# The RWKV preparation of a hybrid diffusion step: sums of squares by dense products, full-width reciprocals, weights asked for earlier

## The reference

```python
kk = heads(k * k_k)
kk = kk / jnp.maximum(jnp.linalg.norm(kk, axis=-1, keepdims=True), 1e-12)
for d in range(2):                       # forward and backward scan
    w_raw = w0[d] + jnp.tanh(wd[:, :, d]) @ w2[d]
    decay = jnp.exp(-jnp.exp(-jax.nn.softplus(-w_raw) - 0.5))
    a = jax.nn.sigmoid(a0[d] + ad[:, :, d] @ a2[d])
    k_d = heads(k * (1 + (a - 1) * k_a))
    y_d, s_d = _wkv7_scan(r_h, decay, k_d, v_h, kk, a, s0, reverse=(d == 1))
```

## Time and profile before

| | |
|---|---|
| median of 3 runs | 2838.48 us |
| the profiled execution | 2838.06 us, span 2836.3 us |
| PE, DVE, ACT busy | 94%, 51%, 25% of the span |
| mean granted TensorE clock | 0.952 of full speed |
| the RWKV part | about 1260 to 1840 us |
| the three scans with a preparation | from about 1377, 1516 and 1660 us |

### The profile page before, as it was taken

How to read it: one execution, slowest core, us unless ns; L and a number is a source line. 1 busy time by engine, 2 the same in 40 slices (tenths; PEclk the granted TensorE clock), 3 DMA queues, 4 the chain that set the end, 5 groups by cost and what they waited for, 6 DMA issues and landing times. The chain is left out here.

```text
span 2836.3 us, 51388 instructions
## 1 busy us (share of the span) xinstructions
PE 2653.5 (94%) x21182; PEld 2520.2 (89%) x21182; DVE 1437.2 (51%) x2751; ACT 703.8 (25%) x1341; POOL 87.6 (3%) x158
## 2 busy tenths in 40 slices
PE   5999999999999799987979797988999999999998
PEld 3999999999999799845767676788999999999998
DVE  4754555555533866217584848444633333333344
ACT  3311111111112311124444444222311111111113
POOL 0000000000000000000202021200000000000000
PEclk8999999999999899987888888999999999999999
DMA  7222222222210222242021212051111111111101
GB/s 281 67 81 78 82 70 83 69 83 83 83 38 1 62 79 94 69 189 65 32 64 40 64 40 65 13 177 44 61 45 38 44 37 44 44 34 40 44 22 68
DMA packets 215861, 192.73 MB, mean 68 GB/s; under 512 B 64755, under 2 KB 184350, under 8 KB 215710
## 3 DMA queue, kind: packets, MB, share of 16 engines
q1 hardware_dynamic: 206224, 165.31, 18.6%
q10 hardware_dynamic: 9486, 25.26, 3.3%
HBM read 158.42 MB, written 32.11 MB: 67 GB/s over the span
## 5 line engine op out<-in xcount | busy, mean ns | idle before, releaser
L129 PE MATMUL ff_ps<-h_hi,ff_wlo 128*128 128x384 f32 x2112 | 715.2, 339 | 7.9 <-DVE h_lo L483 4.7
L130 PE MATMUL ff_ps<-h_lo,ff_whi 128*128 128x384 f32 x2112 | 705.8, 334 | 0.0
L131 PE MATMUL ff_ps<-h_hi,ff_whi 128*128 128x384 f32 x2112 | 705.5, 334 | 0.0
L684 DVE TENSOR_TENSOR ff_s<-ff_ps,ff_s 128x384 f32<-128x384 f32 x132 | 73.6, 557 | 688.6 <-PE ff_ps L131 686.4
L129 PEld LDWEIGHTS ff_ps<-h_hi,ff_wlo 128*128 128x128 f32 x2112 | 396.9, 188 | 11.8 <-DVE h_lo L483 7.8
L130 PEld LDWEIGHTS ff_ps<-h_lo,ff_whi 128*128 128x128 f32 x2112 | 396.9, 188 | 0.0
L131 PEld LDWEIGHTS ff_ps<-h_hi,ff_whi 128*128 128x128 f32 x2112 | 396.5, 188 | 0.0
L129 PE MATMUL ff_ps<-ff_uhi,ff_wlo 128*128 128x384 f32 x1056 | 353.9, 335 | 9.1 <-DVE x L695 9.1
L131 PE MATMUL ff_ps<-ff_uhi,ff_whi 128*128 128x384 f32 x1056 | 352.9, 334 | 0.0
L130 PE MATMUL ff_ps<-ff_ulo,ff_whi 128*128 128x384 f32 x1056 | 352.8, 334 | 0.0
L622 ACT ACTIVATE ff_s<-ff_ps 128x384 f32<-128x384 f32 x132 | 64.9, 492 | 752.8 <-PE ff_ps L131 752.8
(11 more groups left out here) (281 smaller groups left out, 3339.9 us busy)
## 6 DMA issues: line engine op xcount, KB each, us to landing
ff_n<-w_mod ACTq DMA_DIRECT2D x64, 384.0 KB, 3.2
ff_raw<-ffn_w_gate SPq DMA_DIRECT2D x44, 512.0 KB, 4.0
ff_raw<-ffn_w_up SPq DMA_DIRECT2D x44, 512.0 KB, 4.0
ff_raw<-ffn_w_down SPq DMA_DIRECT2D x44, 512.0 KB, 4.5
md_w<-w_mod SPq DMA_DIRECT2D x3, 4096.0 KB, 30.7
pj_raw<-w_in SPq DMA_DIRECT2D x19, 512.0 KB, 4.1
z_dram<-pj_zo SPq DMA_DIRECT2D x15, 576.0 KB, 2.9
rw_rkv<-z_dram SPq DMA_DIRECT2D x12, 576.0 KB, 4.9
```

Source lines behind the costliest of these rows:

```text
L129: pe.matmul(out, w_lo, x_hi, start=start, stop=False)
L130: pe.matmul(out, w_hi, x_lo, start=False, stop=False)
L131: return pe.matmul(out, w_hi, x_hi, start=False, stop=stop)
L684: dve.tensor_tensor(hid[:, t % 2, :], ps[:, 2 + t % 2, 0:CW], silu[:, t % 2, :], ALU.mult)\
```

## The change

`ss_c` becomes one product of the 128x128 block of ones (as loaded operand) with 384 columns of squares. So the sums come out already spread over the 64 channels of their head, 128x384. `wide` and the three `kk_c` items on PE are gone. The clamp, the square root and the reciprocal now work at full width: three clamps of 128x384, one `Sqrt` of 128x1152, three reciprocals of 128x384. The tables are written anew, with `sqrt` in step 5, `inv_0` in slot 1 of step 6, `inv_1` and `inv_2` in the two slots of step 7. SP asks for the small weights behind the block round trip, ahead of `gate_g2` and the big rows. PE and DVE wait for the three rows at the start of every pair's jobs, not of the first alone.

```diff
-PREP_PE = {0: ("a0_0", ), 1: ("a0_1", ), 2: ("ss_0", "ss_1"), 3: ("ss_2", ), 4: ("a0_2", ), 5: ("w0_0", ), 6: ("w0_1", ),
-           7: ("kk_0", ), 8: ("kk_1", ), 9: ("kk_2", ), 10: ("w0_2", ), 11: ("a1_0", ), 12: ("a1_1", ), 13: ("a1_2", ),
-           14: ("w1_0", ), 15: ("w1_1", ), 16: ("w1_2", )}
+PREP_PE = {0: ("a0_0", ), 1: ("a0_1", ), 2: ("ss_0", ), 3: ("ss_1", ), 4: ("ss_2", ), 5: ("a0_2", ), 6: ("w0_0", ), 7: ("w0_1", ),
+           8: ("w0_2", ), 9: ("a1_0", ), 10: ("a1_1", ), 11: ("a1_2", ), 12: ("w1_0", ), 13: ("w1_1", ), 14: ("w1_2", )}
...
             if name.startswith("ss"):
                 self.act_t.wait(pe, "sq")
-                j = int(name[-1])
-                last = head_sums(pe, self.sb, bank, rw.sq[:, :], range(j * NC, (j + 1) * NC))
+                c = int(name[-1])
+                last = pe.matmul(bank[:, 0:CW], self.sb["cst"][:, C_BLK:C_BLK + P], rw.sq[:, c * CW:(c + 1) * CW], start=True, stop=True)
...
-                t.did(name, act.activation(rw.inv[:, :], rw.inv[:, :], ACT.Sqrt))
+                t.did(name, act.activation(rw.sq[:, :], rw.sq[:, :], ACT.Sqrt))
...
-                ins = dve.tensor_scalar(rw.inv[:, six], self.ps[:, self.ITEMS.index(name) % 2, six], 1e-24, None, ALU.max)
+                ins = dve.tensor_scalar(rw.sq[:, cols], self.ps[:, self.ITEMS.index(name) % 2, 0:CW], 1e-24, None, ALU.max)
             elif kind == "inv":
                 self.act_t.wait(dve, "sqrt")
-                ins = dve.reciprocal(rw.inv[:, :], rw.inv[:, :])
-            elif kind == "wide":
-                t.wait(dve, "inv")
-                ins = widen(dve, rw.sq[:, :], rw.inv)
+                ins = dve.reciprocal(rw.sq[:, cols], rw.sq[:, cols])
             elif kind == "kk":
-                self.pe_t.wait(dve, name)
-                ins = dve.tensor_tensor(rw.kk[:, cols], self.ps[:, self.ITEMS.index(name) % 2, 0:CW], rw.kk[:, cols], ALU.mult)
+                t.wait(dve, f"inv_{c}")
+                ins = dve.tensor_tensor(rw.kk[:, cols], rw.sq[:, cols], rw.kk[:, cols], ALU.mult)
...
         back(0)
         back(1)
+        if more:
+            ready.pe_t.wait(sp, Prep.ITEMS[-1])
+            prep.sync_weights(sp)
...
-        else:
-            for sem in ready.z_in:
-                pe.wait_ge(sem, 16)
+        for sem in ready.z_in:
+            pe.wait_ge(sem, 16)
```

More of the change, by code:

```diff
@@ L1297, in others @@
         self.sq = sbuf("sq", [P, T])
-        self.inv = sbuf("inv", [P, 2 * NT])
         self.rkv = sbuf("rkv", [P, 3, T])
@@ L1348 @@
 PP = {n: i for i, n in enumerate(("w0_0", "w0_1", "a0_0", "a0_1", "k_k", "k_a", "r_k", "ln_w", "ln_b", "one_ka"))}
-PREP_PE = {0: ("a0_0", ), 1: ("a0_1", ), 2: ("ss_0", "ss_1"), 3: ("ss_2", ), 4: ("a0_2", ), 5: ("w0_0", ), 6: ("w0_1", ),
-           7: ("kk_0", ), 8: ("kk_1", ), 9: ("kk_2", ), 10: ("w0_2", ), 11: ("a1_0", ), 12: ("a1_1", ), 13: ("a1_2", ),
-           14: ("w1_0", ), 15: ("w1_1", ), 16: ("w1_2", )}
-PREP_ACT = {2: ("kda0_0", ), 3: ("kda0_1", ), 4: ("sqrt", ), 6: ("kda0_2", ), 13: ("kda1_0", ), 14: ("kda1_1", ), 15: ("kda1_2", )}
-PREP_DVE = {3: (("ss_0", "ss_1"), ("kd0_0", )), 4: (("ss_2", ), ("kd0_1", )), 5: ((), ("inv", )), 6: (("wide", ), ()),
[3 rows of a table removed]
+PREP_PE = {0: ("a0_0", ), 1: ("a0_1", ), 2: ("ss_0", ), 3: ("ss_1", ), 4: ("ss_2", ), 5: ("a0_2", ), 6: ("w0_0", ), 7: ("w0_1", ),
+           8: ("w0_2", ), 9: ("a1_0", ), 10: ("a1_1", ), 11: ("a1_2", ), 12: ("w1_0", ), 13: ("w1_1", ), 14: ("w1_2", )}
+PREP_ACT = {2: ("kda0_0", ), 3: ("kda0_1", ), 5: ("sqrt", ), 7: ("kda0_2", ), 11: ("kda1_0", ), 12: ("kda1_1", ), 13: ("kda1_2", )}
+PREP_DVE = {3: (("ss_0", ), ("kd0_0", )), 4: (("ss_1", ), ("kd0_1", )), 5: (("ss_2", ), ()), 6: ((), ("inv_0", )),
[3 rows of a table added]
 class Prep:
@@ L1393, in sync @@
     def sync(self, sp):
-        rw, cols = self.rw, bass.ds(self.p * P, P)
+        rw = self.rw
         for n in (1, 0, 2):
@@ L1397, in sync, with sync_weights @@
               .then_inc(self.z_in[n], 16)
-        for dst, name, sem in ((rw.w2, "decay_w2", self.w_in[0]), (rw.a2, "iclr_a2", self.w_in[1])) * self.weights:
+    def sync_weights(self, sp):
+        cols = bass.ds(self.p * P, P)
+        for dst, name, sem in ((self.rw.w2, "decay_w2", self.w_in[0]), (self.rw.a2, "iclr_a2", self.w_in[1])):
             sp.dma_start(dst[:, :], self.io[name][0].rearrange("d i n -> (d i) n")[:, cols]).then_inc(sem, 16)
@@ L1410, in pe @@
                 self.act_t.wait(pe, "sq")
-                j = int(name[-1])
-                last = head_sums(pe, self.sb, bank, rw.sq[:, :], range(j * NC, (j + 1) * NC))
-            else:
[L1414 to L1421, removed]
-                else:
-                    self.dve_t.wait(pe, "wide")
-                    last = spread(pe, self.sb, bank, rw.sq[:, :], c)
+                c = int(name[-1])
+                last = pe.matmul(bank[:, 0:CW], self.sb["cst"][:, C_BLK:C_BLK + P], rw.sq[:, c * CW:(c + 1) * CW], start=True, stop=True)
+            else:
+                c, d, which = int(name[-1]), int(name[1]), "wa".index(name[0])
+                rows = slice(HS * d, HS * d + HS)
+                if self.weights:
+                    pe.wait_ge(self.w_in[which], 16)
+                last = pe.matmul(bank[:, 0:CW], (rw.w2, rw.a2)[which][rows, :], rw.lora[rows, which, c * CW:(c + 1) * CW],
+                                 start=True, stop=True)
             self.pe_t.did(name, last)
@@ L1467, in dve @@
                 self.pe_t.wait(dve, name)
-                six = slice(c * 2 * NC, (c + 1) * 2 * NC)
-                ins = dve.tensor_scalar(rw.inv[:, six], self.ps[:, self.ITEMS.index(name) % 2, six], 1e-24, None, ALU.max)
+                ins = dve.tensor_scalar(rw.sq[:, cols], self.ps[:, self.ITEMS.index(name) % 2, 0:CW], 1e-24, None, ALU.max)
             elif kind == "inv":
                 self.act_t.wait(dve, "sqrt")
-                ins = dve.reciprocal(rw.inv[:, :], rw.inv[:, :])
-            elif kind == "wide":
-                t.wait(dve, "inv")
-                ins = widen(dve, rw.sq[:, :], rw.inv)
+                ins = dve.reciprocal(rw.sq[:, cols], rw.sq[:, cols])
             elif kind == "kk":
-                self.pe_t.wait(dve, name)
-                ins = dve.tensor_tensor(rw.kk[:, cols], self.ps[:, self.ITEMS.index(name) % 2, 0:CW], rw.kk[:, cols], ALU.mult)
+                t.wait(dve, f"inv_{c}")
+                ins = dve.tensor_tensor(rw.kk[:, cols], rw.sq[:, cols], rw.kk[:, cols], ALU.mult)
             elif kind[:2] == "kd":
@@ L1959, in vector @@
             front.sdve_t.wait(dve, f"M{NCH - 1}_1")
[L1960 to L1963, removed]
+        for sem in ready.z_in:
+            dve.wait_ge(sem, 16)
+        ready.dve_t.wait(dve, f"scan1_{NC - 1}")
         for d in range(2):
```

## The result

The changed kernel takes 2858.06 us (median of 5 runs, 2855.78 to 2861.05), the kernel before beside it 2837.62 (2832.33 to 2844.47): a ratio of 1.0075, with a 95% interval of 1.0055 to 1.0095. It is slower by 20 us. The profiled run is the median one, 2858.06 us with a span of 2856.3, so the two spans (2836.3 and 2856.3) show the same 20 us.

A forecast was written before the change was run, and what follows sets the result against it. PE was busy 94% of the span, scan cost set above all by steps at the low clock. Scans +16.3, first preparation -0.9, added waits +0.3 gave +15.7: about 2853 us; own range 2845 to 2861, whole range 2814 to 2862.

The forecast's parts named there:

- The weights: Step 0 of each scan: PE's waits of 0.97, 1.58 and 1.30 us go; the step takes about 2.75 us.
- Steps 0 to 5 high: Steps 0 to 5 of each scan run at the high clock level and take 13.8 us together.
- The root: Step 5 on ACT: root ready 4.81 us after that step's S; DVE waits 1.3 us in step 6.
- The reciprocals: Steps 6 and 7 on DVE: 1.80 us per 128x384 reciprocal, the two steps taking 9.1 us.
- The clock: Falls between steps 6 and 8 behind PE's gaps; steps 8 to 14 take 25.6 us, 15 and 16 take 6.3.
- The sum of the scans: Each scan takes 54.8 us: +8.6, +3.7 and +4.0 us, together +16.3.
- The first preparation: First pair's preparation, with no scan beside it: its DVE chain ends 0.9 us sooner; bounds -0.9 and 0.
- fast reciprocal: Rival: 0.54 us a reciprocal; 2842 us if the clock falls, about 2805 if it holds; chance 0.10 in equal halves.
- The spread of the runs: The runs' own spread, taken as about 5 us in building the forecast's range.
- slow reciprocal: Rival: 3.4 us for each reciprocal in the scans and first preparation, about 2872 us; chance 0.05.
- The weights are no help: Rival: PE still waits in step 0, +1.0 to 1.6 us a scan, about 2858 us; chance 0.05.
- The clock holds: Rival: steps 8 to 16 stay high, about 19.6 us, a scan takes 42.5, program 2817 us; chance 0.14.

The follow-up runs named there:

- e1: The kernel before with only the early request for the small weights and the added waits: 2819.68 us, ratio 0.9941.
- e9: The kernel before with eleven reciprocals of known width (18 to 1152 elements) ahead of the first preparation: 2859.67 us in one run.
- e4: The changed kernel with each 128x384 reciprocal replaced by a multiply-and-add of the same size giving a constant: 2811.12 us, ratio 0.9895.
- e11: The changed kernel with the reciprocals one to a step, in steps 6, 7 and 8: 2853.56 us, ratio 1.0051.
- e5: The changed kernel with three filler products each in steps 6 and 7: 2846.86 us, ratio 1.0015.
- e7: The changed kernel with three filler products each in steps 6 and 7 and one in each of steps 8 to 14: 2858.79 us, ratio 1.0075.
- e3: The changed kernel with the small weights asked for late, behind the big rows, as before the change: 2871.17 us, ratio 1.0119.
- e12: The kernel before with the early weights and one filler product of 256 columns in step 2: 2810.58 us, ratio 0.9896.
- e6: The changed kernel with one filler product of 256 columns each in steps 8, 9 and 10: 2861.77 us, ratio 1.0083.
- e8: The kernel before, weights still late, with one filler product in each of steps 2 and 3: 2842.96 us, ratio 1.0027.

## Why the prediction came out right, and where it didn't

The forecast was 2853 us, the time is 2858. The mechanism came as told, and the number is closer than its terms: with the measured price of a reciprocal, 2.54 us, in place of 1.80, the prediction's own sum gives 9 us more, 2862, and smaller terms that it had too high, the S and M between the reciprocals and step 8 above all, took 4 of these back. That the number came so near is in part luck. Step by step:

- *The weights.* Right: the wait is gone, step 0 takes 2.67 us (forecast 2.75). By itself it is the best part of the change, 18 us (e1), and only 3.9 of these are the waits of the earlier trace rows.
- *Steps 0 to 5 high.* Right: 13.63 us from S0 to S6 in two scans and 13.98 in the third, forecast 13.8.
- *The root.* Right: it ends 4.84 us behind the S of step 5 (1395.43 - 1390.59), forecast 4.81, and DVE waits 1.38, forecast 1.3. What the prediction left out is that ACT's copy of Y stands behind the root too, and PE waits 0.93 us for it.
- *The reciprocals.* The mechanism was right and the size off: 2.54 us each, where I took 1.80. The step that failed is "continued to 384 that is 216 + 375 x 4.22": it drew a slope over 366 elements from a difference of 38 ns. e9 has 267 ns at 18 where the profile of before had 254, and an error of 13 ns in that difference is a third of the slope. S6 to S8 takes 10.84 instead of 9.1: the three reciprocals are 2.2 us longer than forecast, and the S and the M between them hold them up for 0.3 us each and not 0.48 and 0.47. The repeat count of 8 that the Trainium skill names ("VectorE: DVE Perf Modes", section "Walkthrough: the 8-slice pipeline in each mode") had led to an estimate of 8.3 ns an element and 3.3 us. The measurement doesn't agree with that reading: e9 has 6.25 ns. The truth lies about halfway between that estimate and the slope of the small rows, and I was wrong to say that two rows decide it.
- *The clock.* The fall in step 6 or 7 and the low level to the scan's end came as told: steps 8 to 14 took 25.0 us (25.6), steps 15 and 16 took 6.35, 5.76 and 6.35 (6.3). That the reciprocals bring on the fall is shown by e4 for two scans of three, that DVE's time and not its placing counts by e11. My reason, gaps in PE, is borne out in part (e5). The gaps were not as I had them, "longer than the 1.58 and 1.30 us, three in a row": they are 0.93, 1.67, 0.49 and 1.06 us, and in all three scans the fall came in the second. That items w and a don't bring the clock back, and that the spread products which stood there are gone, fits all profiles without added fillers; but products over 128 rows are not enough for it, since in e7 such a filler beside the item of every step left the clock low for 27 to 34 us. What lifts it is left open.
- *The sum of the scans.* +19.1 for a forecast of +16.3: 3 x 1.74 for the reciprocals, less 3 x 0.6 for step 8, where Y's products were done before the late S (3.00 us, not 3.66), less 0.6 elsewhere (steps 0 to 5, and 15 and 16 of the second scan).
- *The first preparation.* The sign was wrong: -0.9 forecast, +0.7 measured. It ends 2.00 us later, and 1.29 of these were there before it began (DVE's first memset starts at 1262.03 against 1260.74), which leaves +0.7. The three reciprocals take 7.38 us there and not 5.4, 2.0 more; that alone turns -0.9 into +1.1, and what follows them was 0.4 shorter than I had it. The bounds of -0.9 and 0 held only at the price of 1.80, as the text said; with both ends of that price they would have been -4.7 and +3.9. The rival "fast reciprocal" leaves this out: its 2842 and 2805 lack the 3.8 us that the first preparation would have been shorter.
- *The spread of the runs.* The range was built with "about 5 us"; 28 runs of the kernel before lie between 2821.71 and 2847.02.

The rival "slow reciprocal" named the direction at 2872; 2.54 us is 0.46 of the way to its 3.4. "The weights are no help" gave 2858, the time measured, for a reason that e1 and e3 refute. "The clock holds" was not seen in any profiled scan with the wide reciprocals, and without them one scan of three still fell (e4).

## What to carry to other kernels

A reciprocal on VectorE is to be priced per element of a row, and kept narrow: here 128x18 and a spread through TensorE (0.27 us and nine products, in steps of 2.0 to 2.7 us at the high clock) beat three of 128x384 (7.6 us). A queue that runs in order and carries one link of a recurrence has no room for an instruction longer than a step, wherever in the step it is put. A change with two parts should be timed by parts: here one was worth -18 us and the other +38, and e12 keeps the first alone and adds a filler. Buy a filler where the clock is still high (0.54 us here); at the low clock it is paid in full (1.15 us) and needn't lift it. And one profile is one draw: where the clock of a scan falls in one run and not in the next, take several runs, and say which of them was profiled.

## What the runs showed of the hardware

- RECIPROCAL, f32, 128 partitions: 153 ns and 6.25 ns per element from 18 to 1152 elements, against 0.35 us for a multiply and add of 128x384 between the same rows.
- Whether the clock falls is uneven between scans with the same instructions: e4's third scan fell and its first two didn't, e1's likewise; e9's second scan held, behind a wait of 1.60 us, and its third, behind one of 1.35, fell; and e5's ten runs of one kernel range over 28 us with a mean clock of 0.948 to 0.959. e12's four range over 3.
- The clock can stay at 1.2 GHz while PE shows no idle time at all: for 34.1 us in e7, with a 256-column filler in most of its steps, and for 27.3 us in the kernel before.
- Outside e6 and e7 it came back, in 23 low stretches of 23 in the scans, in the second step in which a spread product, a dense sum or a filler stood alone in the place of an item w or a (step 3 once, else step 8 or 16; twice up to 0.1 us before that step began). Whether those products are the reason is not shown.
- The late weight's wait differs between profiles of the same instructions: 0.97 us and 2.73 us in the first scan (before, and e8), and 3.93 us in e9, where that scan begins 24 us later.
